# Moving three VectorE products of the RWKV stages to GpSimd, and running the last head pair of stick-breaking from its last tile to its first

## The reference

```
S = S * w_t + (S @ -kk_t) (kk_t * a_t)^T + v_t k_t^T ;  y_t = S @ r_t
y = groupnorm(y) + sum(r * k * r_k) * v ;  yA * SiLU(zA)
```

## Time and profile before

| | us |
|---|---|
| median of three runs | 5440.93 |
| the profiled execution | 5420.49 |
| its span, first to last instruction | 5418.9 |
| TensorE busy | 4867.8 |
| VectorE busy | 2093.7 |
| ScalarE busy | 1546.3 |
| GpSimd busy | 123.9 |
| mean granted clock of TensorE | 0.951 of 2.4 GHz |

### The profile page before, as it was taken

One profiled execution on the slowest core, in us unless ns is written; L12 is line 12 of the kernel. 1 busy time (PEld: TensorE's weight loads), 2 busy tenths in 40 slices (PEclk: granted clock), 3 DMA queues, 4 the chain that ended last, 5 costly groups with the idle time before them and its releaser, 6 DMA issues. The chain is left out here.

```text
span 5418.9 us, 64262 instructions
## 1 busy us (share of the span) xinstructions
PE 4867.8 (90%) x24624; PEld 3189.0 (59%) x24624; DVE 2093.7 (39%) x4616; ACT 1546.3 (29%) x3518; POOL 123.9 (2%) x370
## 2 busy tenths in 40 slices
PE   6989898788989979999969898987889899799999
PEld 2657667456756655555426566674567566555554
DVE  2455555335534440111124555553355344401111
ACT  2333332335533330000023322323355334300000
POOL 0000000000000000000000000000000000000000
PEclk8999999889989989999989999999999899899999
DMA  5100101210012111211140101002100121111111
GB/s 197 23 13 18 30 9 17 77 48 13 21 49 71 52 39 44 72 64 41 55 158 23 13 18 30 9 17 77 48 19 15 49 73 50 53 35 67 64 41 58
DMA packets 132706, 253.25 MB, mean 47 GB/s; under 512 B 51444, under 2 KB 86516, under 8 KB 126918
## 3 DMA queue, kind: packets, MB, share of 16 engines
q1 hardware_dynamic: 132280, 244.32, 14.0%
q10 hardware_dynamic: 112, 4.72, 0.2%
HBM read 201.66 MB, written 52.06 MB: 47 GB/s over the span
## 5 line engine op out<-in xcount | busy, mean ns | idle before, releaser
L2353 PE MATMUL banks<-hT,w_gate 128*128 128x384 f32 x2304 | 772.0, 489 | 16.0 <-DMA w_branch<-in_w_br 16.0
L2353 PEld LDWEIGHTS banks<-hT,w_gate 128*128 128x128 f32 x2304 | 440.1, 191 | 323.9 <-DMA w_branch<-in_w_br 16.4
L958 PE MATMUL banks<-hT,w_piece 128*128 128x384 f32 x1536 | 563.9, 510 | 5.8 <-ACT raw L1062 5.6
L2120 PE MATMUL banks<-hT,w_piece 128*128 128x384 f32 x1152 | 390.9, 495 | 17.5 <-DMA w_piece<-in_w_cols 16.0
L958 PEld LDWEIGHTS banks<-hT,w_piece 128*128 128x128 f32 x1536 | 287.9, 198 | 182.2 <-issue 26.8
L2357 PE MATMUL banks<-y_branch,w_branch 128*128 128x384 f32 x1152 | 395.1, 486 | 0.0
L2378 ACT ACTIVATE gate_tanh<-banks 128x384 f32<-128x384 f32 x144 | 70.7, 491 | 1066.0 <-PE banks L2357 1066.0
L2120 PEld LDWEIGHTS banks<-hT,w_piece 128*128 128x128 f32 x1152 | 217.1, 193 | 172.0 <-issue 20.4
L2357 PEld LDWEIGHTS banks<-y_branch,w_branch 128*128 128x128 f32 x1152 | 218.9, 190 | 152.6
L2391 DVE SCALAR_TENSOR_TENSOR gate_tanh<-gate_tanh,banks 128x384 f32<-128x384 f32 x96 | 53.2, 554 | 634.2 <-ACT gate_tanh L2378 634.2
L2369 PE MATMUL banks<-w_out,mergedT 128*128 128x512 f32 x576 | 247.5, 592 | 0.0
(11 more groups left out here) (335 smaller groups left out, 7982.4 us busy)
## 6 DMA issues: line engine op xcount, KB each, us to landing
w_piece<-in_w_cols SPq DMA_DIRECT2D x68, 512.0 KB, 4.3
w_ada<-in_w_ada SPq DMA_DIRECT2D x12, 2048.0 KB, 9.8
w_gate<-in_w_cols SPq DMA_DIRECT2D x48, 512.0 KB, 3.4
y_branch<-y_gated SPq DMA_DIRECT2D x18, 768.0 KB, 10.2
w_branch<-in_w_br SPq DMA_DIRECT2D x48, 256.0 KB, 3.5
sb_cached_keysT<-in_sbkT SPq DMA_DIRECT2D x8, 1024.0 KB, 6.7
sb_cached_values<-in_sbv SPq DMA_DIRECT2D x8, 1024.0 KB, 5.2
w_out<-in_w_out SPq DMA_DIRECT2D x16, 512.0 KB, 5.0
```

The source lines that it names most:

```text
L958: last = mm(dst, w[0 if kind in ("k", "v") else 1][:, k, :], hT[:, k, c], start=(k == 0), stop=(k == KD - 1))
L2120: last = mm(ps[:, bank[n], 0:TG], w[wn % 3][:, k, :], hT[:, k, TG * g:TG * g + TG], start=(k == 0), stop=(k == KD - 1))
L2353: nc.tensor.matmul(ps[:, 2 * (u % 4), 0:TG], wg[j % 2][:, k, :], hT[:, k, c], start=(k == 0), stop=(k == KD - 1))
```

## The change

The state's decay, the product of z with its sigmoid, and the bonus leave VectorE's list, and GpSimd gets a list in the fused stages. GpSimd makes the product of z first (when ScalarE has the sigmoid), then the decayed state of each chunk behind `s_scaled`, and behind the one of chunk 12 the bonus. VectorE waits for `sd_made` ahead of L1187 and for `z_gated` ahead of the first `gate`; ScalarE waits for `z_gated` before it reuses `t[2]`. The decay was a product with a per-partition scalar; on GpSimd it is a product of two tensors, the second one broadcast from one column.

In the last head pair of stick-breaking the prompt tiles go 7, 6, ..., 0 in place of 0, 1, ..., 7, behind the sample tile as before. The column ranges and the order of the last pair's stores follow.

```diff
@@ rwkv_fused
+        @block.gpsimd
+        def _(pool):
+            G = nc.gpsimd
+            if scan:
+                pool.wait_ge(z_sigmoid, 1)
+                G.tensor_tensor(R.zs[h % 2][:, :], R.zs[h % 2][:, :], t[2][:, :], ALU.mult).then_inc(z_gated, 1)
+            for n in range(NCK):
+                if scan and n + 1 < NCK:
+                    pool.wait_ge(s_scaled, n + 3)
+                    G.tensor_tensor(SD[:, :], ST[:, :], R.pend[h % 2][:, n + 1:n + 2].broadcast_to([P, P]), ALU.mult).then_inc(sd_made, 1)
+                if prep and n == 12:
+                    pool.wait_ge(shifted, 3)
+                    released(pool, "bs", 1)
+                    released(pool, "bs", 2)
+                    G.tensor_tensor(R.bonus[nx % 2][:, :], rT[:, :], vT[:, :], ALU.mult)
@@ scalar, chunk 2
                         act.wait_ge(shifted, 1)
+                        if scan:
+                            act.wait_ge(z_gated, 1)
@@ vector, chunk n
                     dve.wait_ge(s_ready, n + 2)
+                    if n >= 1:
+                        dve.wait_ge(sd_made, n)
                     for hh in range(2):
                         hc = slice(64 * hh, 64 * hh + 64)
                         ins = V.scalar_tensor_tensor(ST[hc, hc], ps[hc, 6, hc], R.pend[h % 2][hc, n:n + 1], SD[hc, hc], ALU.mult, ALU.add)
                     own(ins, s_scaled)
-                    if n + 1 < NCK:
-                        own(V.tensor_scalar(SD[:, :], ST[:, :], R.pend[h % 2][:, n + 1:n + 2], None, ALU.mult))
                 latent_gates(n)
-                if scan and n == 1:
-                    dve.wait_ge(z_sigmoid, 1)
-                    own(V.tensor_tensor(R.zs[h % 2][:, :], R.zs[h % 2][:, :], t[2][:, :], ALU.mult))
...
                     if n == 12:
                         shift("v", vT)
-                        released(dve, "bs", 1)
-                        released(dve, "bs", 2)
-                        own(V.tensor_tensor(R.bonus[nx % 2][:, :], rT[:, :], vT[:, :], ALU.mult))
...
                 if scan and n == 11:
+                    dve.wait_ge(z_gated, 1)
                     gate(0, 7, 384)
@@ stick_breaking
+SB_UNITS_LAST = SB_UNITS[:2] + [("p", i, hh) for i in reversed(range(NPT)) for hh in range(2)]
...
-    units = [(h, *unit) for h in range(HP) for unit in SB_UNITS]
+    units = [(h, *unit) for h in range(HP - 1) for unit in SB_UNITS] + [(HP - 1, *unit) for unit in SB_UNITS_LAST]
+
+    def tile_cols(h, j):
+        if j == 0:
+            return slice(TP, T)
+        i = j - 1 if h < HP - 1 else NPT - j
+        return slice(P * i, P * i + P)
...
-                sp.wait_ge(gated, (NPT + 1) * h + (4, 7, 9)[part])
+                sp.wait_ge(gated, (NPT + 1) * h + ((4, 7, 9)[part] if h < HP - 1 else (9, 6, 3)[part]))
...
-                store_rows(h, 0)
+                if h < HP - 1:
+                    store_rows(h, 0)
...
-                store_rows(h, 1)
-            store_rows(HP - 1, 2)
+                if h < HP - 1:
+                    store_rows(h, 1)
+            for part in (2, 1, 0):
+                store_rows(HP - 1, part)
...
-                    c = slice(TP, T) if j == 0 else slice(P * (j - 1), P * j)
+                    c = tile_cols(h, j)
```

More of the change, by code:

```diff
@@ L843, in rwkv_fused @@
              "state_out", "u_ready", "u_added", "y_ready", "y_copied", "s_ready", "s_scaled",
-             "stat_in", "stat_out", "y_normed", "y_turned", "y_gated", "y_stored", "g_sigmoid", "g_made", "g_stored", "vec", "act_own")
+             "stat_in", "stat_out", "y_normed", "y_turned", "y_gated", "y_stored", "z_gated", "sd_made", "g_sigmoid", "g_made", "g_stored", "vec", "act_own")
     with S.stage(*names) as (block, sb, (w0_loaded, w1_loaded, par_done, fill_ready, free0, free1, summed, exps_done,
@@ L847, in rwkv_fused @@
                                          state_out, u_ready, u_added, y_ready, y_copied, s_ready, s_scaled,
-                                         stat_in, stat_out, y_normed, y_turned, y_gated, y_stored, g_sigmoid, g_made, g_stored, vec, act_own)):
+                                         stat_in, stat_out, y_normed, y_turned, y_gated, y_stored, z_gated, sd_made, g_sigmoid, g_made, g_stored, vec, act_own)):
         free = (free0, free1)
```

## The result

The changed kernel takes 5379.3 us (median of 4 runs, 5364.88 to 5382.55) beside 5434.52 us of the kernel before on the same chip: the ratio is 0.9887, with a 95% interval of 0.9869 to 0.9905. A second set of runs gave 5368.59 us and 0.9872 (0.9857 to 0.9888). The forecast was 5398.5 us, in a range of 5372 to 5424; the second set's median lies 3 us under that range. Its profiled execution took 5382.55 us, 5380.9 of it span: 38 us less than the profiled execution of before, where the sum of the steps said 42.4.

A forecast was written before the change was run, and what follows sets the result against it. TensorE was busy for 90% of the span, so only work taken off VectorE where TensorE waits pays. Stick-breaking's 32 us plus the fused stages' 10.4 made 42.4, off the 5440.9 median: 5398.5 us, range 5372 to 5424.

The forecast's parts named there:

- Part 1, the decayed state: Decay moved to GpSimd: 1.4 us less per stage that scans and prepares, 1.0 per stage that only scans.
- first rival: Bonus really free, chunk 13's wait 1.3 us; waits of 1.5 to 1.7 bring no clock fall: 5374 us, chance 0.12.
- rival 4: Fused stages: GpSimd becomes the bound; a 3.2 us round trip cancels the gain, 3.7 decides for slower; chance 0.04.
- Part 2, z: z's product on GpSimd: 1.0 us less in each of the two stages that only scan, 0 with preparation.
- Part 3, the bonus: Bonus on GpSimd, 2.6 us, delays chunk 12's sums: a 0.33 us loss per stage; TensorE's wait stays 3 us.
- the far branch: The tiny L1127 is held by GpSimd's bonus too: +0.45 us per stage, 0.7 us more over six stages.
- Fused stages, sum: All fused stages together, decay, z's product and bonus: 10.4 us less.
- Part 4, the order: Stick-breaking's last pair, tiles descending: ends 16 us sooner in each layer, 32 us in two layers.
- the 1 us that I gave as a sign: Stick-breaking's last pair: VectorE's waits under 1 us from tile 4 down would show the forecast.
- rival 2: Stick-breaking's descent runs at half clock: two layers save only 16 to 20 us, kernel at 5414; chance 0.15.

The follow-up runs named there:

- e12: The kernel before with only z's product moved to GpSimd: 5413.21 us, ratio 0.9984 to the kernel before.
- e6: The kernel before, untouched, profiled a second time: 5423.48 us (one execution).
- e11: The changed kernel with the decayed state back on VectorE, z's product and the bonus still on GpSimd: 5385.28 us, ratio 0.9931 to the kernel before.
- e9: The changed kernel with GpSimd's bonus one chunk later, behind the decayed state of chunk 13, second run: 5331.77 us, ratio 0.9804 to the kernel before.
- e8: The changed kernel with the last pair's tiles in order 7, 6, 0, 1, 2, 3, 4, 5: 5373.55 us, ratio 0.9885 to the kernel before.
- e1: The kernel before with only the new order of stick-breaking's last head pair: 5404.12 us, ratio 0.9939 to the kernel before.
- e2: The changed kernel with the old order of stick-breaking, so GpSimd's part alone: 5397.14 us, ratio 0.9936 to the kernel before.
- e3: The changed kernel with the bonus back on VectorE at its old place, first run: 5348.12 us, ratio 0.9848 to the kernel before.
- e10: The changed kernel with the bonus back on VectorE at its old place, second run: 5357.27 us, ratio 0.9856 to the kernel before.
- e4: The changed kernel with GpSimd's bonus behind the decayed state of chunk 13, first run: 5332.44 us, ratio 0.9819 to the kernel before.
- e5: The changed kernel, untouched, run again: 5368.59 us.
- e7: The changed kernel with GpSimd making the decayed state five times over in the stages that only scan: 5385.64 us (one execution).

## Why the prediction was right

**Part 1, the decayed state: the sum right, its terms less so, one effect missed.** In the stages that prepare I summed 1.4 us: 0.29 net in each of three chunks and 0.19 in each of three more. Measured, before less after: 0 to 1 0.32, 3 to 4 0.34, 6 to 7 0.28, 7 to 8 and 8 to 9 0.09 each, 9 to 10 and 10 to 11 0.13 each: 1.38. So the chunks with a long list of VectorE gave only 0.09 to 0.13, and 10 to 11, which I hadn't counted, made up for part of it: that the sum is met to 0.03 us is in part luck. In the stages that only scan I said 1.0, and it was 1.5 (0.46, 0.33, 0.33, 0.33; 0.13 of the first is z's, by e12): nothing was eaten by GpSimd there. The wait on `sd_made` costs nothing: 0.65 us from TensorE to the update, as before. Missed: before, TensorE waited 1.70 us in 9 to 10, and the fills that followed ran slow in three of six stages (five of six in e6). Now it waits 1.56 us, and they never do; that is 1.31 us each. Before in the second such stage, then after in the third:

```profile
586.90 0.49 PE L1007 MATMUL banks<-bk_and_vu_rows 128*128 128x128 f32 x2 [1.70 <-DVE bk_and_vu_rows L1183]
...
587.62 4.49 PE L958 MATMUL banks<-hT,w_piece 128*128 128x384 f32 x8
```

```profile
806.09 0.49 PE L1023 MATMUL banks<-bk_and_vu_rows 128*128 128x128 f32 x2 [1.56 <-DVE bk_and_vu_rows L1201]
...
806.80 2.80 PE L974 MATMUL banks<-hT,w_piece 128*128 128x384 f32 x8
```

My first rival said that waits of 1.5 to 1.7 us were followed by no fall of the clock. That holds for 1.53 and 1.56 us and not for 1.70, in the very trace that I had. e11, where the state alone is back on VectorE, brings back the 1.70 us and the slow fills (four of six stages), so the state's move is the cause of the 1.31 us. That the length of this one wait is what decides fits all runs, but none varies it alone.

How GpSimd's product meets a long VectorE instruction shows behind chunk 0, where a scan of two tensors runs:

```profile
339.60 2.56 DVE L1214 TENSOR_TENSOR_SCAN temp<-k_shifted,temp 128x1152 f32<-128x1152 f32 x1
339.64 2.71 POOL L935 TENSOR_TENSOR state_decayed<-state,decay_of_chunk 128x128 f32<-128x128 f32 x1 [21.93 <-DVE state L1207]
```

Here GpSimd is the one that waits: it ends 0.19 us behind the scan, and 0.40 us become 2.71. Such meetings, with the scan or with a shorter product, lengthen 38 of the 120, and they are the reason for the mean of 649 ns above; the other 82 take 0.40 us. It cost nothing, for in these chunks the fills leave the state more than 4 us. I had it the other way round, GpSimd slipping in behind the first instruction; rival 4, with 3.7 us as the point where the sum turns, was nearer than my 0.5 to 1.15 us made it look.

**Part 2, z: right.** 1.0 us forecast in each of the two stages, 1.01 measured (3.27 to 2.26), and by e12 too, though there 0.18 of it is given back by chunk 6.

**Part 3, the bonus: right, at the far branch.** Forecast 2.6 us on GpSimd, measured 2.615 (x8); forecast +0.33 us, between 0.21 if the tiny L1127 passes and 0.45 if it is held. It is held (2.10 us for 0.17), and the interval 12 to 13 grew by 0.44 at like clock (7.40 to 7.84, 7.71 to 8.15), 2.65 us over the six stages. This is the branch by the Trainium skill (SBUF — State Buffer, SBUF: two separate sides), whose rule counts such single-input instructions among those that take the lock: the trace agrees, down to a tile of six columns. The estimate of 2.5 us for 1152 columns from the Trainium skill (GPSIMD Engine Reference, Elementwise — side-by-side cycle accounting) was 0.1 short. The drop of the clock stayed, and came in the sixth stage as well (5.88 us where it had been 4.20). The rival that made the bonus free fell. But its price was right: e9, where the bonus really costs nothing, is 37 us faster. In the chunks of the six stages it is 26.3 us (465.1 to 438.8), where I had 24; 3.2 more lie in the two stages that only scan, where the edit does nothing, and the rest is `rwkv_solve`.

**Fused stages, sum.** 6 x (1.38 - 0.44) + 2 x (1.5 + 1.0) = 10.6, forecast 10.4; with the clock's part (3 x 1.31 won in 10 to 11, 0.8 lost in 13 to 14, 0.6 in the last interval of one stage) 13.1; the profiles differ by 12.9.

**Part 4, the order: right, nearly term by term.** VectorE begins tile 5 29.8 us behind the first scores (forecast 31.0). From there to its last product 33.7 us (28.5 + 4.6). Tail from 1992.54 to 1994.63, 2.1 us (2.0). The pair's end comes 16.4 us sooner in relation to its start (forecast 16). VectorE's waits from tile 4 down are 1.43, 0.33, 0.79, 0.79 and 1.10 us, two of them over the 1 us that I gave as a sign; together 4.4, where I had 4.6. What the text didn't say is where the gain lies; by e8 most of it is the fills' place, and little the descent. That the descent would run at half clock (rival 2) fell: 0.81 on average from 1958.85 to 1992.54, better than the 0.70 that I had assumed.

**The sum against the median: the term that was too small.** The steps gave 42.4 us, the edited places of the two profiles 45.5, the medians 55 and 69 us (5434.52 - 5379.3, 5437.66 - 5368.59). So 13 to 27 us are not in the sum, and that the first set lies within the range is owed to the range's width, not to a term for them; the second lies just under it. They go with GpSimd's part and not with the order: e1 gives 33 us where I had 32, e2 40 where I had 10.4.

Where they lie, fourteen profiles show in part. Four have both the state and the bonus on VectorE as before (before, e6, e12, e1). One piece is in the edited stages themselves, ahead of what I summed: from a scanning stage's first matmul to the update of chunk 0. These eight heads together take 235.9, 244.0, 249.5 and 251.9 us in the four (mean 245), and 223.8 to 236.9 in the ten others (mean 232): 13 us. TensorE has next to no pause in them, and what differs is the granted clock; the second and the third scanning stage of before:

```profile
509.82:538.23 28.41, 28.33 (x88) 13.84 (x89) 12.37 (x23) 8.01 (x13) 0.00 (x0) 0.95 0.00 1
718.87:752.79 33.92, 33.92 (x88) 16.44 (x89) 12.33 (x23) 8.01 (x13) 0.00 (x0) 0.77 0.00 1
```

The other piece is in stages without an edit. The four have latent pairs at 380 us or more in six of eight layers, the ten others in one of twenty: 8 us on average over both layers. Latent attention is at 156 us in four of eight and in six of twenty. `rwkv_solve` goes the other way by 3 us. Why these should follow what was changed is not shown: e12 with z alone has the long heads (249.5), and e11 with the state back and e3 and e10 with the bonus back have the short ones (223.8, 233.1, 233.2), so no single move explains them. It stays open.

## What to carry to other kernels

Work moved to an idle GpSimd was free here where VectorE waited or worked out of PSUM, and not beside VectorE's work on SBUF tiles; find such a stretch in the timeline and put the work there, for one chunk's difference was worth 37 us here. Price a wait of TensorE with what follows it: here a wait of 3 us was mostly followed by 1.3 to 2.9 us more in slow matmuls. Place TensorE's filler beside the tiles whose other engines work longest, before any finer reordering.

## What the runs showed of the hardware

- A product of one 128x6 tile with a constant waits on VectorE for a whole GpSimd product of two tensors, 2.10 us in place of 0.17; a reduction of 128x384 does not (0.55), nor does an addition that reads PSUM (0.29).
- It goes both ways: GpSimd's 128x128 product took 2.71 us beside VectorE's scan of 2.56.
- Waits of TensorE in 12 to 13 and the six intervals behind them, in stages with the same fills: 1.53 us, never slow (e4, e9); 2.92, slow in three of six (e3 and e10 alike); 3.02, 23 of 24 (before, e6, e12, e1); 3.46, 30 of 30 (after, e5, e2, e7, e8); 3.55, six of six (e11). In 10 to 11, behind waits of 1.70 us, 21 of 30 (before, e6, e12, e1, e11); behind 1.56, none of 54 (the other nine).
- Untouched stages have two or more lengths, by the granted clock of a few matmuls: latent pairs 373 to 376 or 380 to 381 us, latent attention 151 or 156, modulation 73.3 to 77. The head of a scanning stage that also prepares takes 27.0 to 29.5 us at a granted clock of 0.91 or more, or 32.9 to 34.3 at 0.79 or less. A difference of 5 us in one stage of two single profiles is not yet an effect of an edit.
